# A two-layer decoder step on one core: the turning of queries and keys one unit later, class scores in one round, and near scores of blocks 4 to 7 with 32 stationary columns in four column groups

## The chip, the cores and the metric

The kernel runs on 1 core of one Trainium2 chip. The metric is the time on the device of one execution, in microseconds; lower is better. Engines are named as in the profile: PE is TensorE (PEld its weight loads), DVE is VectorE, ACT is ScalarE, POOL is GpSimd, SP is SyncE, which starts the DMAs.

## The reference

Two layers are applied to a prompt of 1024 tokens and to 8 single tokens of a sample group, with a model width of 1024, 8 attention heads and 8 mLSTM heads of 64 each. Per layer:

```
h = rmsnorm(x); z = h @ w_in            # q, k, v of 8 attention heads, q, k, v, gate of 8 mLSTM heads
for (window, dilation) in ((128, 1), (512, 4), (2048, 16)):
    s = q @ k.T * HEAD_DIM ** -0.5      # keys at distance 0 .. window, in steps of dilation
    m = max(s); e = exp(s - m); l = sum(e); o = e @ v / l
o_a = the three o, merged by their denominators
h_b = chunkwise mLSTM with matrix memory
x += concat(rmsnorm(o_a), sigmoid(o_gate) * rmsnorm(h_b)) @ w_out
x += ConvGLU(rmsnorm(x)); x += sigmoid(rmsnorm(x) @ w_ple_gate) * (p @ w_ple_proj)
```

The change touches `s = q @ k.T` of the prompt and the steps that bring q and k into the layout which it needs.

## The kernel before

Everything stays in one program; each engine has its own list of instructions, written out by hand in Python, and they meet through counting semaphores. There is no scheduler: the order on an engine is the order in which its function issues.

**Products.** The combined projection `h @ w_in` is made for one pair of heads at a time. For pair p there are nine tiles of tokens (eight of 128 prompt tokens, and one with the 8 sample tokens) and eight k-steps each, so 72 k-steps. A k-step is three matmuls over split operands (L1001, L1002, L1003: low times high, high times low, high times high); for the ninth tile of most pairs it is two small ones (L1010, L1012). ScalarE copies a finished tile out of PSUM into `zt` (`z_evac`), which raises `z_done`.

**Attention.** Pairs 0 to 3 hold attention heads. The loop `for p in range(PAIRS): for u in range(NU)` runs over 16 units per pair. Unit u stands for query block u // 2 (128 tokens) and head u % 2 of the pair, so even units have e = 0 and odd ones e = 1. While the units of pair p run, the 72 k-steps of pair p + 1 are dealt out over them (`FILL`: 8, 8, 8, then 4 each, 2 in the last two units), in two halves around the attention steps. In an odd unit PE first issues `scores` of the next query block, for both heads. Then come products, `turn_back` (L1191) and, at the end, `turn_p` (L1160); in an even unit products, `turn_p` and `values` (L1179, L1184) of the block before.

**Scores.** Query blocks 0 to 3 are scored against all keys up to their own block (L1150). Blocks 4 to 7 are scored against two near blocks of 128 keys (L1150, 256 columns) and against class keys: every fourth key, queries and keys sorted into four residue classes. Each class is a matmul with 32 stationary columns (queries) that writes 32 partitions (L1145); four classes and two heads make a round of eight. `class_keys` is 128 for blocks 4 and 5, 224 for block 6 and 256 for block 7, and a round takes at most 128 of them. `q3` is stored with the 128 queries of a block sorted by class, so a slice of 32 is one class; `k3` is stored in order and read with `r:P:4`. The operands are fp32, and each matmul leaves two records in the trace.

**From scores to values.** VectorE adds the mask and takes the maximum (`masked`, L2172, L2174), ScalarE makes the exponentials (`probabilities`, L1690), PE turns them (`turn_p`), VectorE copies them back (`near`, L2182), PE multiplies by the values. `scores` waits for `s_masked`, `turn_p` for `p_done` and for `pt0` of the unit before.

**Norm and turn.** Before `scores` of pair p, its q and k are normed, rotated and turned by PE (`turn_third`, L1106), a third of the eight tiles at a time: thirds 0 and 1 (three tiles each) during the units of the pair before, third 2 (two tiles) during its own. `norm_part` gives VectorE's three steps of the norm (`norm_squares`, `norm_scale`, `norm_rope`, the last instruction of which is L2095) to units 4 to 6 for third 0 and 9 to 11 for third 1. `turn_part` gives the turn of q (j = 0) and that of k (j = 1) to a unit each; in an even unit the turn stands between the two halves of the products, in an odd one at the unit's end. Both use PSUM bank 3. The q turn waits for `qk_norm` and until the bank is emptied of the k turn before (`k_evac`, VectorE's copy L2103); the k turn waits until ScalarE's copy of q (L1679, `q_evac`) is done.

Of the kernel before, what the change touches and what calls it, by code (L numbers as in the profile page):

```python
# [16 lines left out]
P = 128  # L17
# [9 lines left out]
HD = 64  # L27
# [28 lines left out]
def tok(t):  # L56
    return slice(t * P, t * P + rows(t))
# [7 lines left out]
def col(c):  # L65
    return slice(c * CH, (c + 1) * CH)
# [75 lines left out]
def class_keys(qb):  # L142

    return 0 if qb < NDENSE else P if qb < 6 else 32 * (qb + 1)


def near_keys(qb):

    return range(qb + 1) if qb < NDENSE else range(qb - 1, qb + 1)
# [13 lines left out]
def score_bank(g):  # L163

    return g % 3
# [31 lines left out]
def turn_part(p, u):  # L197

    if p == 0 and u in (2, 3):
        return 0, 1, u - 2  # L200
    if u in (6, 7):
        return p, 2, u - 6
    if p + 1 < PAIRS:
        for x, a in enumerate((8, 12)):
            if u in (a, a + 1):
                return p + 1, x, u - a
    return None
# [7 lines left out]
def turned_value(p, half):  # L215

    return 3 * p + half + 1 if p < PAIRS else 3 * PAIRS + 2 * (p - PAIRS) + half + 1
# [61 lines left out]
def tiles(first, last):  # L279
# [9 lines left out]
    s_ready=32, s_masked=64, p_done=64, t0_ready=64, pt0=64, o_ready=32, oc_done=32, ob_ready=32, o_read=32,  # L289
# [45 lines left out]
def build(nc, A, O):  # L335
    with ExitStack() as ctx:
# [3 lines left out]
        def sem(name):  # L340
            return ctx.enter_context(nc.semaphore(name))
# [88 lines left out]
        ps = ctx.enter_context(nc.psum_tensor("ps", [P, 8, 512], F32))  # L430
# [24 lines left out]
        def score_mask(qb):  # L455
# [24 lines left out]
        s_ready, s_masked, p_done, t0_ready, pt0, o_ready, oc_done, ob_ready, o_read = [sem(n) for n in (  # L480
            "s_ready", "s_masked", "p_done", "t0_ready", "pt0", "o_ready", "oc_done", "ob_ready", "o_read")]
# [126 lines left out]
        def one_hot(h, n, g=0):  # L608

            return ident[32 * g:32 * g + NH, 32 * g + h:32 * g + h + 1].to_broadcast([NH, n])  # L610

        def row_part(g, j):

            return rowr[32 * g:32 * g + NH, j * 512:(j + 1) * 512]
# [384 lines left out]
        def _(pe):  # L999
            def three(out, a_hi, a_lo, b_hi, b_lo, first, last):  # L1000
                nc.tensor.matmul(out, a_lo, b_hi, start=first, stop=False)  # L1001
                nc.tensor.matmul(out, a_hi, b_lo, start=False, stop=False)  # L1002
                return nc.tensor.matmul(out, a_hi, b_hi, start=False, stop=last)  # L1003
# [47 lines left out]
            for t in range(5):  # L1051
                turn_x(t)
                if t == 1:
                    n = DEPTH * 3 * KT
# [5 lines left out]
            for l in range(DEPTH):  # L1060
# [69 lines left out]
                def scores(p, qb):  # L1130

                    if qb % 3 == 0:
                        pe.wait_ge(*at(q_evac, turned_value(p, qb // 3)))
                        pe.wait_ge(*at(k_evac, turned_value(p, qb // 3)))
                    g = NU * p + 2 * qb
                    if g >= 2:
                        pe.wait_ge(*at(s_masked, g - 1))
                    q3, k3 = qkA[p % 2]
                    n = class_keys(qb)
                    for a in range(0, n, P):  # L1140
                        b = min(n, a + P)
                        for r in range(4):
                            for e in range(2):
                                h = slice(HD * e, HD * e + HD)
                                mm = nc.tensor.matmul(ps[32 * r:32 * r + 32, score_bank(g + e), a:b].rearrange("p (t i) -> p t i", i=32),  # L1145
                                                      q3[h, qb, 32 * r:32 * r + 32], k3[h, a // 32:b // 32, r:P:4], start=True, stop=True)
                    own = near_keys(qb)
                    for e in range(2):
                        h = slice(HD * e, HD * e + HD)
                        mm = nc.tensor.matmul(ps[:, score_bank(g + e), n:n + len(own) * P].rearrange("p (t n) -> p t n", n=P), q3[h, qb, :],  # L1150
                                              k3[h, own.start:own.stop, :], start=True, stop=True)
                    mm.then_inc(s_ready, 1)
# [59 lines left out]
                products(0, KT * NT + 4, NPROD)  # L1212
                pe.wait_ge(*at(z_done, NT))
                scores(0, 0)
                pe.wait_ge(*at(k_evac, 1))
                for p in range(PAIRS):
                    for u in range(NU):
                        e, qb = UNITS[u]
                        if e and qb + 1 < NT:
                            scores(p, qb + 1)  # L1220
                        elif e and p + 1 < PAIRS:
                            scores(p + 1, 0)
                        part = turn_part(p, u)
                        before = (p, qb - 1) if qb else (p - 1, NT - 1)
                        half = (ahead(u) + ahead(u + 1)) // 2
                        products(p + 1, ahead(u), half)
                        if e == 0:
                            if part:
                                turn_third(*part)
                            products(p + 1, half, ahead(u + 1))  # L1230
                            turn_p(p, u)
                            if before[0] >= 0:
                                values(*before)
                        else:
                            if half == ahead(u + 1):
                                turn_p(p, u)
                            if before[0] >= 0:
                                turn_back(*before)
                            if half < ahead(u + 1):
                                products(p + 1, half, ahead(u + 1))  # L1240
                                turn_p(p, u)
                            if part:
                                turn_third(*part)
# [48 lines left out]
                for q in range(PAIRS):  # L1292
                    p = PAIRS + q
# [39 lines left out]
                    for e in range(2):  # L1333
                        for j in range(2):
                            mm = nc.tensor.matmul(ps[HD * e:HD * e + HD, 3 + j, :], one_hot(2 * q + e, HD, j), row_part(j, j),
                                                  start=True, stop=True)
# [5 lines left out]
                    for j in range(2):  # L1342
                        for e in range(2):
                            mm = nc.tensor.matmul(ps[:, ((0, 1), (2, 5))[e][j], :], one_hot(2 * q + e, P, 2 * e + j),
                                                  row_part(2 * e + j, j), start=True, stop=True)
# [7 lines left out]
                    for c in range(NT):  # L1353
                        g = NT * q + c
                        next_products(ahead_b(q, c), ahead_b(q, c + 1))
                        pe.wait_ge(*at(ws_done, g + 1))
                        if c >= 2:
                            pe.wait_ge(*at(c_upd, 9 * q + c))
                        mm = nc.tensor.matmul(ps[:, (2, 5)[c % 2], 0:2 * (HD + 1)],
                                              att[:, 3 * SEQ + 512 + (c % 2) * P:3 * SEQ + 512 + (c % 2 + 1) * P],  # L1360
                                              zt[:, p % 2, c, VO:OG], start=True, stop=True)
# [4 lines left out]
                        if q + 2 == PAIRS and c == 0:  # L1366
                            pe.wait_ge(*at(kq_used, 3 * NB))
                            for r in range(3):
                                mm = nc.tensor.transpose(ps[0:HD, 0, (r + 1) * P:(r + 2) * P], sall[:, r, :, :].rearrange("p b h -> p (b h)"), ident[:, :])
# [5 lines left out]
                        for e in range(2):  # L1375
                            zc = VO + e * (HD + 1)
                            a = 3 * SEQ + (c % 2) * 256 + e * P
                            nc.tensor.matmul(ps[:, 3 + c % 2, e * (HD + 1):(e + 1) * (HD + 1)], att[:, a:a + P],  # L1378
                                             zt[:, p % 2, c, zc:zc + HD + 1], start=(e == 0), stop=False)
                        if q + 1 == PAIRS and c + 1 == NT:  # L1380
# [3 lines left out]
                                         Cst, start=False, stop=True).then_inc(n_ready, 1)  # L1384
# [31 lines left out]
                for c in range(3):  # L1416
# [3 lines left out]
                    for o in range(KT):  # L1420
# [7 lines left out]
                        for k in range(KT):  # L1428
                            w_h, w_l = weights(B + B_OUT + o // 2, k, 256, (o % 2) * P, P)
                            mm = three(ps[:, 4 + j % 3, 0:CH], w_h, w_l, hi[:, k, col(c)], lo[:, k, col(c)], k == 0, k == KT - 1)  # L1430
# [80 lines left out]
                for j in range(24):  # L1511
                    b, c, o = j // 6, (j % 6) // 2, j % 2
# [8 lines left out]
                    for k in range(KT):  # L1521
                        w_h, w_l = weights(B + B_PLE + 2 * b, k, 256, o * P, P)
                        mm = three(ps[:, j % 3, 0:CH], w_h, w_l, hi[:, k, col(c)], lo[:, k, col(c)], k == 0, k == KT - 1)
# [10 lines left out]
                    for k in range(2):  # L1534
                        w_h, w_l = weights(B + B_PLE + 2 * b + 1, k, 256, o * P, P)
                        mm = three(ps[:, 3 + j % 3, 0:CH], w_h, w_l, ph[:, k, col(c)], pl[:, k, col(c)], k == 0, k == 1)
# [5 lines left out]
            for t in range(NT + 1):  # L1542
# [4 lines left out]
                for k in range(KT):  # L1547
                    mm = nc.tensor.transpose(ps[0:m, 2 * (t % 2) + k // 4, (k % 4) * P:(k % 4 + 1) * P], X[:, k, tok(t)], ident[:, :])
# [1206 lines left out]
```

## Time and profile before

| | us |
|---|---|
| median of 3 runs | 3154.49 |
| lowest and highest | 3153.2, 3158.83 |
| the profiled execution, its own time | 3152.16 |
| its span in the trace | 3150.4 |
| TensorE (PE) busy | 3071.9 (98%) |
| VectorE (DVE) busy | 1823.9 (58%) |
| ScalarE (ACT) busy | 982.0 (31%) |
| mean granted TensorE clock, share of full speed | 0.993 |

The durations below come from that one execution. Its own time is 2.3 us under the median of the runs, its span another 1.8 us less, since the span goes from the first instruction to the last one alone. The attention part of the first layer lies at about 70 to 345 us of the span, that of the second at 1622 to 1900 us.

### The profile page before, as it was taken

What the parts mean: (1) busy time and instruction counts of PE and PEld (TensorE: products, weight loads), DVE (VectorE), ACT (ScalarE), POOL (GpSimd) and SP (SyncE); (2) the same over time, 40 slices, a digit from 0 to 9 for tenths busy, and PEclk for the clock granted to TensorE, in tenths of its full rate; (3) what the DMA queues carried; (4) which work ended last, traced back from release to release, by engine and by line L of the source; (5) the groups of instructions that cost most, each with busy time, mean ns of one, the idle gap of its engine ahead of it and who ended that gap; (6) DMA issues with size and microseconds to landing.
All of it is one profiled execution on the core that took longest, in us unless ns stands there. A gap on an engine that the chain in (4) does not pass through costs nothing.

```text
span 3150.4 us, 52020 instructions
## 1 busy us (share of the span) xinstructions
PE 3071.9 (98%) x20099; PEld 2809.9 (89%) x20099; DVE 1823.9 (58%) x4369; ACT 982.0 (31%) x2053; POOL 899.0 (29%) x2061
## 2 busy tenths in 40 slices
PE   7999999899999999999999999998999999999998
PEld 7877677599999999999997777767999999999998
DVE  5675465755555555557577745646555555555663
ACT  4333244533111111115333333454321111111251
POOL 3112023414223233223422211323223243223231
PEclk8999999999999999999999999999999999999999
DMA  6222133611111111110231222336111111111111
GB/s 186 71 62 55 46 101 112 198 44 63 43 41 41 55 53 41 54 41 24 94 88 49 58 55 59 115 103 191 54 41 41 66 43 46 49 41 41 41 38 72
DMA packets 242335, 213.95 MB, mean 68 GB/s; under 512 B 41988, under 2 KB 221124, under 8 KB 240496
## 3 DMA queue, kind: packets, MB, share of 16 engines
q1 hardware_dynamic: 242088, 210.62, 22.0%
q8 instruction: 159, 2.61, 0.3%
q14 instruction: 88, 0.72, 0.1%
HBM read 178.95 MB, written 31.61 MB: 67 GB/s over the span
## 4 chain that ended last, share of the span: by engine, by line
PE 85%; DVE 9%; ACT 2%; issue 1%; DMA 1%; SPq 1%; POOL 0%; DVEq 0%; ACTq 0%
PE ps L1001 25%; PE ps L1003 25%; PE ps L1002 25%; PE ps L1184 1%; PE ps L1160 1%; DVE att L2182 1%; PE ps L1150 1%; PE ps L1145 1%; PE ps L1179 1%; PE ps L1281 1%; PE ps L1305 1%; DVE lo L2017 1%; DVE att L2172 1%; PE ps L1378 1%; DVE zt L2088 1%
## 5 line engine op out<-in xcount | busy, mean ns | idle before, releaser
L946 POOL TENSOR_TENSOR wlo<-raw,whi 128x128 fp32r<-128x128 f32 (+3 forms) x1952 | 855.4, 484 | 1780.5 <-ACT whi L1570 1382.2
L1001 PE MATMUL ps<-hi,wlo 128*128 128x344 f32 x2880 | 924.3, 321 | 1.9 <-DVE X L2522 1.3
L1003 PE MATMUL ps<-hi,whi 128*128 128x344 f32 x2880 | 919.5, 319 | 0.0
L1002 PE MATMUL ps<-lo,whi 128*128 128x344 f32 x2880 | 918.6, 319 | 0.0
L1001 PEld LDWEIGHTS ps<-hi,wlo 128*128 128x128 f32 x2880 | 541.6, 188 | 5.0 <-issue 2.2
L1003 PEld LDWEIGHTS ps<-hi,whi 128*128 128x128 f32 x2880 | 541.1, 188 | 0.0
L1002 PEld LDWEIGHTS ps<-lo,whi 128*128 128x128 f32 x2880 | 540.2, 188 | 0.6
L1001 PE MATMUL ps<-whi,lo 128*128 128x512 f32 (+3 forms) x1056 | 413.7, 392 | 6.5 <-ACT zt L1645 4.5
L1003 PE MATMUL ps<-whi,hi 128*128 128x512 f32 (+3 forms) x1056 | 390.4, 370 | 0.0
L1002 PE MATMUL ps<-wlo,hi 128*128 128x512 f32 (+3 forms) x1056 | 389.0, 368 | 0.0
L2601 DVE TENSOR_TENSOR X<-X,ps 128x344 f32<-128x344 f32 x528 | 268.3, 512 | 184.5 <-PE ps L1003 182.6
L1912 ACT ACTIVATE wb<-wb 128x344 f32<-128x344 f32 x132 | 64.9, 492 | 967.3 <-DVE wb L2588 967.3
L1001 PE MATMUL ps<-yhi,wlo 128*128 128x344 f32 x1056 | 339.9, 322 | 0.7 <-DVE X L2601 0.7
L1003 PE MATMUL ps<-yhi,whi 128*128 128x344 f32 x1056 | 338.3, 320 | 0.0
L1002 PE MATMUL ps<-ylo,whi 128*128 128x344 f32 x1056 | 337.4, 319 | 0.0
L1001 PEld LDWEIGHTS ps<-whi,lo 128*128 128x128 f32 (+1 forms) x1056 | 197.1, 187 | 68.5 <-issue 26.2
L1003 PEld LDWEIGHTS ps<-whi,hi 128*128 128x128 f32 (+1 forms) x1056 | 196.8, 186 | 26.6
L2580 DVE TENSOR_TENSOR wa<-ps,rstd 128x344 f32<-128x344 f32 x132 | 68.2, 517 | 258.1 <-PE ps L1003 257.7
L1002 PEld LDWEIGHTS ps<-wlo,hi 128*128 128x128 f32 (+1 forms) x1056 | 197.8, 187 | 20.2
L1570 ACT ACTIVATE whi<-raw 128x2048 fp32r<-128x2048 f32 (+3 forms) x106 | 188.1, 1782 | 43.1 <-DMA raw<-in_w_down 33.3
L1001 PEld LDWEIGHTS ps<-yhi,wlo 128*128 128x128 f32 x1056 | 198.7, 188 | 1.5 <-DVE X L2601 1.3
L1002 PEld LDWEIGHTS ps<-ylo,whi 128*128 128x128 f32 x1056 | 198.3, 188 | 0.2
(331 smaller groups left out, 3746.7 us busy)
## 6 DMA issues: line engine op xcount, KB each, us to landing
raw<-in_w_up SPq DMA_DIRECT2D x44, 1024.0 KB, 5.0
raw<-in_w_in SPq DMA_DIRECT2D x112, 256.0 KB, 4.3
raw<-in_w_down SPq DMA_DIRECT2D x22, 1024.0 KB, 4.8
kvb<-in_cache_win_k SPq DMA_DIRECT2D x48, 256.0 KB, 3.0
cache<-in_cache_win_v SPq DMA_DIRECT2D x42, 256.0 KB, 4.0
X<-x_scratch SPq DMA_DIRECT2D x4, 2064.0 KB, 11.5
raw<-in_w_out SPq DMA_DIRECT2D x8, 1024.0 KB, 8.9
raw<-in_w_ple_gate SPq DMA_DIRECT2D x8, 1024.0 KB, 4.9
```

What stands on the lines that cost most here:

```text
L946: pool.tensor_tensor(out=wlo[:, s, r], in0=raw[:, s, r], in1=whi[:, s, r].bitcast(F32), op=ALU.subtract).then_inc(w_split, 1)
L1001: nc.tensor.matmul(out, a_lo, b_hi, start=first, stop=False)
L1002: nc.tensor.matmul(out, a_hi, b_lo, start=False, stop=False)
L1003: return nc.tensor.matmul(out, a_hi, b_hi, start=False, stop=last)
L1145: mm = nc.tensor.matmul(ps[32 * r:32 * r + 32, score_bank(g + e), a:b].rearrange("p (t i) -> p t i", i=32), q3[h, qb, 32 * r:32 * r + 32], ...
L1150: mm = nc.tensor.matmul(ps[:, score_bank(g + e), n:n + len(own) * P].rearrange("p (t n) -> p t n", n=P), q3[h, qb, :], k3[h, own.start:own ...
L1160: mm = nc.tensor.transpose(ps[0:n, 4, j * P:(j + 1) * P], score_place(g)[:, a:a + n], ident[:, :])
L1179: nc.tensor.matmul(ps[HD * e:HD * e + HD, 6, 32 * r:32 * r + 32], class_values(c, r)[0:n, e * HD:(e + 1) * HD], turned_place(g + e)[0:n, a ...
L1570: do(nc.scalar.activation(whi[:, s, 0:used], raw[:, s, 0:used], ACT.Copy), w_hi, wait=False)
L1912: do(nc.scalar.activation(w, w, ACT.Gelu_apprx_tanh), gelu_done, wait=False)
L2580: do(v.tensor_tensor(out=w[:, 2:CH + 2], in0=ps[:, s % 3, 0:CH], in1=rstd[:, col(c)], op=ALU.mult), gate_read)
L2601: do(v.tensor_tensor(out=x, in0=x, in1=ps[:, 5 + (24 * i + j) % 3, 0:CH], op=ALU.add), dn_read, wait=False)
```

## The change

Three edits. The turns of thirds 0 and 1 of the next pair's q and k go from units 8 and 9, 12 and 13 to units 9 and 10, 13 and 14. In `scores`, the class keys of a query block go through in one round of up to 256 columns, where there was one round for each 128. And for query blocks 4 to 7 the near scores are made by eight matmuls, each with the 32 queries of a class as stationary columns, where there were two with all 128; the moving columns, the 256 near keys, stay the same for all of them, and so does what is written where.

```diff
--- before.py
+++ after.py
@@ -201,7 +201,7 @@
     if u in (6, 7):
         return p, 2, u - 6
     if p + 1 < PAIRS:
-        for x, a in enumerate((8, 12)):
+        for x, a in enumerate((9, 13)):
             if u in (a, a + 1):
                 return p + 1, x, u - a
     return None
@@ -1137,14 +1137,21 @@
                         pe.wait_ge(*at(s_masked, g - 1))
                     q3, k3 = qkA[p % 2]
                     n = class_keys(qb)
-                    for a in range(0, n, P):
-                        b = min(n, a + P)
+                    if n:
                         for r in range(4):
                             for e in range(2):
                                 h = slice(HD * e, HD * e + HD)
-                                mm = nc.tensor.matmul(ps[32 * r:32 * r + 32, score_bank(g + e), a:b].rearrange("p (t i) -> p t i", i=32),
-                                                      q3[h, qb, 32 * r:32 * r + 32], k3[h, a // 32:b // 32, r:P:4], start=True, stop=True)
+                                nc.tensor.matmul(ps[32 * r:32 * r + 32, score_bank(g + e), 0:n].rearrange("p (t i) -> p t i", i=32),
+                                                 q3[h, qb, 32 * r:32 * r + 32], k3[h, 0:n // 32, r:P:4], start=True, stop=True)
                     own = near_keys(qb)
+                    if n:
+                        for r in range(4):
+                            for e in range(2):
+                                h = slice(HD * e, HD * e + HD)
+                                mm = nc.tensor.matmul(ps[32 * r:32 * r + 32, score_bank(g + e), n:n + len(own) * P].rearrange("p (t n) -> p t n", n=P),
+                                                      q3[h, qb, 32 * r:32 * r + 32], k3[h, own.start:own.stop, :], start=True, stop=True)
+                        mm.then_inc(s_ready, 1)
+                        return
                     for e in range(2):
                         h = slice(HD * e, HD * e + HD)
                         mm = nc.tensor.matmul(ps[:, score_bank(g + e), n:n + len(own) * P].rearrange("p (t n) -> p t n", n=P), q3[h, qb, :],
```

On PE's queue, at the end of unit 13 and in unit 14 of pair 0, this stood before (L1160 is `turn_p`, L1010 and L1012 the ninth tile's products, L1106 the turn, here that of k):

```order
L1012 MATMUL ps<-wlo,hi 8x384
L1160 MATMUL ps<-ident,att 128x128
L1160 MATMUL ps<-ident,att 96x128
L1160 MATMUL ps<-ident,att 128x128 x2
L1106 MATMUL ps<-ident,zt 128x128 x3
L1010 MATMUL ps<-whi,thin 40x384
L1012 MATMUL ps<-wlo,hi 8x384
L1010 MATMUL ps<-whi,thin 40x384
L1012 MATMUL ps<-wlo,hi 8x384
```

The same place now (the later lines of the file are 7 further down, so `turn_p` is L1167):

```order
L1012 MATMUL ps<-wlo,hi 8x384
L1167 MATMUL ps<-ident,att 128x128
L1167 MATMUL ps<-ident,att 96x128
L1167 MATMUL ps<-ident,att 128x128 x2
L1106 MATMUL ps<-ident,zt 128x128 x3
L1010 MATMUL ps<-whi,thin 40x384
L1012 MATMUL ps<-wlo,hi 8x384
L1106 MATMUL ps<-ident,zt 128x128 x3
L1010 MATMUL ps<-whi,thin 40x384
L1012 MATMUL ps<-wlo,hi 8x384
```

The first L1106 is now the turn of q, which stood in the middle of unit 12 before, and the second, one k-step behind it, is the turn of k.

The scores of query block 7 of pair 0 on PE, with the last values ahead of them (L1184 and L1179 are `values`, L1145 the class scores, L1150 the near scores), before:

```order
L1160 MATMUL ps<-ident,att 128x128 x2
L1184 MATMUL ps<-att,zt 64x128 x2
L1179 MATMUL ps<-att 64x32 x8
L1184 MATMUL ps<-att,zt 64x128 x2
L1145 MATMUL ps<-zt 32x128 x16
L1150 MATMUL ps<-zt 128x256 x2
L1010 MATMUL ps<-whi,thin 40x384
```

And now (L1191 and L1186 are `values`, L1144 the class scores, L1151 the near scores):

```order
L1167 MATMUL ps<-ident,att 128x128 x2
L1191 MATMUL ps<-att,zt 64x128 x2
L1186 MATMUL ps<-att 64x32 x8
L1191 MATMUL ps<-att,zt 64x128 x2
L1144 MATMUL ps<-zt 32x256 x8
L1151 MATMUL ps<-zt 32x256 x8
L1010 MATMUL ps<-whi,thin 40x384
```

Two rounds of class scores with 128 keys became one with 256, and the two near matmuls of 128 stationary columns became eight of 32.

## Rows read from the trace of the kernel before

**Rows 1.** The page: TensorE's busy time, share and instructions.
```profile
PE 3071.9 (98%) x20099; PEld 2809.9 (89%) x20099; DVE 1823.9 (58%) x4369; ACT 982.0 (31%) x2053; POOL 899.0 (29%) x2061
```

**Rows 2.** Busy time by stretch: span, PE, PEld, DVE, ACT, POOL, clock, DMA.
```profile
70.00:345.00 275.00, 264.43 (x2233) 212.09 (x2232) 174.05 (x513) 99.44 (x266) 60.75 (x142) 0.99 0.22 58
```

**Rows 3.** PE's waits: what waited for whom, us in total, times, longest.
```profile
PE ps L1106 <- DVE zt L2095: 10.6, 6, 1.8
...
PE ps L1106 <- DVE zt L2103: 6.6, 4, 2.0
...
PE ps L1106 <- DVE kT L2103: 2.4, 2, 1.2
```

**Rows 4.** Timeline of PE, unit 12 of pair 1: start, duration, instruction.
```profile
194.31 0.33 PE L1003 MATMUL ps<-whi,hi 128*128 128x384 f32 x1
196.41 0.55 PE L1106 MATMUL ps<-ident,zt 128*128 128x128 f32 x3 [1.77 <-DVE zt L2095]
196.72 0.42 PE L1001 MATMUL ps<-whi,lo 128*128 128x384 f32 x1
```

**Rows 5.** Timeline of PE, unit 8 of pair 0.
```profile
110.80 0.34 PE L1003 MATMUL ps<-whi,hi 128*128 128x384 f32 x1
...
112.72 0.42 PE L1001 MATMUL ps<-whi,lo 128*128 128x384 f32 x1
```

**Rows 6.** Timeline of PE, around a q turn that waits for nobody.
```profile
88.27 0.34 PE L1003 MATMUL ps<-whi,hi 128*128 128x384 f32 x1
...
88.69 0.42 PE L1001 MATMUL ps<-whi,lo 128*128 128x384 f32 x1
```

**Rows 7.** Timeline of PE, unit 8 of pair 2.
```profile
243.24 0.34 PE L1003 MATMUL ps<-whi,hi 128*128 128x384 f32 x1
...
245.85 0.42 PE L1001 MATMUL ps<-whi,lo 128*128 128x384 f32 x1
```

**Rows 8.** Timeline of PE, end of unit 13 and unit 14 of pair 1.
```profile
203.09 0.49 PE L1106 MATMUL ps<-ident,zt 128*128 128x128 f32 x3
203.33 0.42 PE L1010 MATMUL ps<-whi,thin 128*40 128x384 f32 x1
...
203.77 0.33 PE L1010 MATMUL ps<-whi,thin 128*40 128x384 f32 x1
```

**Rows 9.** Timeline of ACT: its copy of the q turn of rows 4.
```profile
197.00 0.49 ACT L1679 ACTIVATE zt<-ps 128x384 f32<-128x384 f32 x1 [3.42 <-PE ps L1106]
```

**Rows 10.** Timeline of DVE: near(7) of pairs 0 and 2, near(12) of pair 2.
```profile
111.28 0.69 DVE L2182 COPY att<-ps 128x512 f32<-128x512 f32 x1
...
244.41 0.69 DVE L2182 COPY att<-ps 128x512 f32<-128x512 f32 x1
...
268.17 0.69 DVE L2182 COPY att<-ps 128x512 f32<-128x512 f32 x1 [2.37 <-PE ps L1184]
```

**Rows 11.** Busy time by stretch, behind the stall of pair 2 (columns as rows 2).
```profile
246.00:250.00 4.00, 4.00 (x26) 3.39 (x25) 1.86 (x6) 1.94 (x5) 4.00 (x10) 0.57 0.02 4
```

**Rows 12.** Timeline of PE, scores of blocks 5 and 7 of pair 1.
```profile
180.45 1.09 PE L1184 MATMUL ps<-att,zt 128*64 128x128 f32 x16
181.48 0.66 PE L1145 MATMUL ps<-kT,rstd 64*32 64x128 f32 x16
182.07 0.70 PE L1150 MATMUL ps<-kT,rstd 64*128 64x256 f32 x4
182.70 0.44 PE L1001 MATMUL ps<-whi,lo 128*128 128x384 f32 x1
...
199.43 1.12 PE L1145 MATMUL ps<-kT,rstd 64*32 64x128 f32 x32
200.48 0.70 PE L1150 MATMUL ps<-kT,rstd 64*128 64x256 f32 x4
```

**Rows 13.** Timeline of PE, scores of block 3 of pair 0 (512 columns).
```profile
98.34 1.13 PE L1150 MATMUL ps<-zt 64*128 64x512 f32 x4
99.40 0.44 PE L1001 MATMUL ps<-whi,lo 128*128 128x384 f32 x1
```

## Prediction

> **What bounds the kernel now.** I read the page first: TensorE is busy for 98% of the span [rows 1], so a change counts where it takes work or idle time off TensorE. The changed lines run in the attention part of each of the two layers alone; in the first that is 70 to 345 us, where PE is busy 264.43 of 275 us, so 10.6 us idle [rows 2]. The table of waits says before what it idles: L1106, the turning of a third of q or k, waited 10.6 + 6.6 + 2.4 = 19.6 us in 12 waits, each time for VectorE [rows 3]. That is nearly all of PE's idle time in both attention parts. The timeline shows where. In unit 12 of pair 1 (the q turn of third 1) PE issues its last product at 194.31, L1106 starts at 196.41, released by the rope step L2095, and the next product at 196.72 [rows 4]. In unit 8 of pair 0 (third 0) it is 110.80 to 112.72 [rows 5]; there the wait is for the copy L2103 that empties bank 3.
>
> **The change, part by part. (a) Later turns.** A q turn that waits for nobody takes, from the last product before it to the first behind it, 88.69 - 88.27 = 0.42 us [rows 6]. The stalled ones take 196.72 - 194.31 = 2.41 and 112.72 - 110.80 = 1.92 us, and the one in unit 8 of pair 2 takes 245.85 - 243.24 = 2.61 us [rows 7]: 1.99, 1.50 and 2.19 us too much. A layer has three of the first kind, two like the second, one like the third: 3 x 1.99 + 2 x 1.50 + 2.19 = 11.2, and two layers 22.3 us. (It is more than 19.6 because a restart costs 0.2 us beyond the idle time that the table counts.) Are the operands there later? The rope step was done 2.1 us after PE had got to unit 12; the new place, the end of unit 13, where the k turn stands now, lies at 203.09, 6.7 us behind the old one [rows 4, 8]. Third 0 moves as far, and was 1.5 to 2.2 us short. Yes, with much to spare.
>
> What is late next? First, the k turn. It needs bank 3 emptied by ScalarE, and it now stands in the middle of unit 10 or 14, close behind its q turn. ScalarE's copy starts 0.04 us after the turn ends (196.41 + 0.55, then 197.00) and takes 0.49 [rows 4, 9]; with 0.04 for the hand-over back, the bank is free 0.57 us after a turn's end. In unit 10 two k-steps stand in between, six products of 384 columns, at 2.4 GHz at least 0.96 us: no wait. In unit 14 it is one k-step of the ninth tile, two matmuls from 203.33 to 203.77, beside a turn whose modelled end is 203.09 + 0.49 = 203.58 [rows 8]. So the k turn is up at 203.77 and may start at 203.58 + 0.57 = 204.15. That is 0.38 us of wait; 0.11 of it would have gone into its own fill (0.42 us unstalled against 196.72 - 196.41 = 0.31), so 0.27 is lost, in 3 pairs of 2 layers 1.6 us (bounds 0, if the copy hides, and 3.2, at twice that). Behind it in PE's queue wait turn_p(14) and the values of block 6, and near(14) on VectorE waits for turn_p. VectorE's copy of k moves ahead of near(14), whose input comes later anyway.
>
> Second, VectorE. In pair 2 PE would reach turn_p(8), which needs near(7), seven products behind 243.24, at 244.36; near(7) ends at 244.41 + 0.69 = 245.10 [rows 7, 10]: 0.7 us of stall remain, 1.4 in two layers (bounds 0 and 2.8). In pair 0 PE would be there at 110.80 + 1.12 = 111.92, and near(7) ends at 111.28 + 0.69 = 111.97: nothing to speak of. Behind the stall of unit 12 VectorE waits 2.37 us for PE (268.17) [rows 10], so PE may come 2 us earlier there, and the k copy that moves down by a unit (about 0.5 us) fits as well.
>
> Third, the clock. Behind the stall of pair 2 the granted clock is 0.57 over 246 to 250 us [rows 11], a stretch at 1.2 instead of 2.4 GHz; (1 - 0.57) x 4 = 1.7 us of full-speed work went there. Without the idle time ahead of it I count that as gained (bounds 0 and 1.7).
>
> (a) sums to -22.3 + 1.6 + 1.4 - 1.7 = -21.0 us.
>
> **(b) Class scores in one round.** Block 7 has 256 class keys, two rounds now, block 6 has 224. A block with one round of 128 takes 182.07 - 181.48 = 0.59 us, the two rounds of block 7 take 200.48 - 199.43 = 1.05 [rows 12]: 0.46 for 128 columns more, 3.6 ns each, and 0.59 - 0.46 = 0.13 us constant. So the second round costs about what its columns cost, if the streaming bounds it. One round of 256 has the same columns: 0 us, though 128 fewer matmuls are issued. Bounds: 0, and a whole constant saved in each of 16 merged blocks, -2.1.
>
> **(c) Near scores with 32 stationary columns.** Now two matmuls of 256 columns take 182.70 - 182.07 = 0.63 us [rows 12], of 512 columns 99.40 - 98.34 = 1.06 [rows 13]. So 256 columns are 0.43 us (four passes at 2.4 GHz with both heads side by side) and 0.20 is a constant, the change of form and the first load of 128 columns. Afterwards eight matmuls stream the 256 columns in eight tiles, right behind class rounds of the same form, whose constant is paid already. The two ends: if all eight tiles stream side by side at full rate, near costs 0.43, that is 0.20 less; if they run at the class rounds' rate, 256 x 3.6 ns = 0.92, 0.29 more. The trace has no near score of this form. The class rounds take 3.6 ns a column where full rate would be 1.67, and differ from L1150 in two ways: eight tiles instead of two, and keys read at every fourth element instead of in a row. That the reading is at fault is suggested by L1184, which splits the array into two column groups and reads unbroken rows: its 16 records, eight matmuls of four passes of 128 columns, take 181.48 - 180.45 = 1.03 us [rows 12], and two full-rate streams would need 0.85. I take -0.20 in 4 blocks x 4 pairs x 2 layers = 32 blocks: -6.4 us; the other end is +9.3.
>
> The Trainium skill, "SBUF — State Buffer", Specifications (TRN2), says that a 16-byte line must be hit at least twice for full bandwidth; every fourth fp32 element hits each line once. By that rule the class rounds are slow through their stride and the near rounds would not be: the sum would be the one I take. By the class row alone it would be 15.7 us longer.
>
> Sum: -21.0 + 0 - 6.4 = -27.4 us on the profiled execution's 3152.16, so 3124.8. The median shown, 3154.49, is 2.3 higher: 3127.
>
> **Rivals.** R1: eight tiles don't keep full rate, (c) is +9.3, and the time 3154.5 - 21.0 + 9.3 = 3143. For it: the only rounds of this form in the trace run at that rate. Against it: the stride.
> R2: the stall moves. Units 8 and 12 are freed, but turn_p, turn_back or the k turns wait for VectorE or ScalarE in its place, and half of (a) comes back, 10 us: 3137. For it: the 0.7 us of pair 2. Against it: VectorE's idle 2.37 us behind the old stall.
> R3, slower: the four column groups of the near scores, which all read the same key columns, stream one after the other. Then near costs 4 x 0.43 + 0.1 = 1.8 us instead of 0.63, 32 x 1.18 = +38 us: 3154.5 - 21.0 + 38 = 3171. It decides once near takes over 0.63 + 21.0/32 = 1.29 us. Against it: eight class matmuls of four passes of 128 columns would need 0.85 us in that way, and take 0.46 beside their constant.
>
> **How the numbers follow.** Forecast 60% (its own range 3121 to 3134), R1 23%, R2 12%, R3 3%, others 2%. The range for 8 in 10 has to reach R1: 3119 to 3145. Two tenths of a per cent, what a measurement here can tell from no change, are 6.3 us, so faster means below 3148, which holds for the forecast, R2 and most of R1: 0.92; same 0.05 (R1 together with R2); slower 0.03.
>
> **What would show it.** L1106's waits fall from 19.6 us to under 4, all in unit 14 and ended by ScalarE. From the first class record to the first product behind the near scores it is 0.59 + 0.63 = 1.22 us for a block with 128 class keys: 1.02 by the forecast, 1.5 by R1, 2.4 by R3; for block 7, 1.68: 1.5, 2.0, 2.9. The drop of the clock at 246 us is gone. I am wrong in (a) if L1160 or L1191 wait more than 3 us more, in (c) if the scores take longer than now.

## The result, and the profile after

The changed kernel takes 3132.88 us (median of 4 runs, 3131.01 to 3135.49), the one before in the same comparison 3155.98 (median of 4, 3153.2 to 3158.83). The ratio is 0.993, its 95% interval 0.9917 to 0.9942: 22 us faster by the ratio, 23.1 by the medians. The forecast was 3127, with 3119 to 3145 as the range.

The page of the profiled execution: span, then busy time, then the chain that ended last by engine.

```profile
span 3133.7 us, 52276 instructions
...
PE 3068.3 (98%) x20227; PEld 2808.6 (90%) x20227; DVE 1824.9 (58%) x4369; ACT 980.6 (31%) x2053; POOL 900.0 (29%) x2061
...
PE 88%; DVE 6%; ACT 2%; DMA 2%; issue 1%; SPq 1%; POOL 0%; DVEq 0%; ACTq 0%
```

PE's busy time fell by only 3.6 us against [rows 1], the span by 16.7; most of what went was idle time. The two attention parts, busy time by stretch (columns as in [rows 2]):

```profile
70.00:335.00 265.00, 262.58 (x2315) 212.14 (x2315) 175.94 (x516) 99.23 (x267) 61.76 (x140) 1.00 0.23 60
1617.00:1883.00 266.00, 263.51 (x2352) 211.95 (x2351) 174.98 (x515) 99.82 (x268) 56.17 (x128) 1.00 0.23 60
```

PE is idle 2.4 us of 265, where it was 10.6 of 275 [rows 2]. Measured from the first turn of a layer (L1106) to the first instruction behind its attention part, the part takes 276.7 us instead of 290.0 in the first layer and 276.8 instead of 288.6 in the second, 25.0 us less in all. That is more than the 16.7 us by which the profiled spans differ. Some 8 us of this one execution went elsewhere. The first turn started 2.5 us later. From the end of the first attention part to the first turn of the second layer 5.5 us more passed; in that stretch PE waited 4.9 us at once for L2404, which stood behind a load of in_state_C (2.1 us before, and at most 2.4 to 4.0 us in other kernels here that don't change that code). The other 2.7 us of the stretch are not traced to a cause. The medians, 23.1 us apart, don't show that loss.

PE's waits, whole run (who waited for whom, us in total, times, longest):

```profile
PE ps L1366 <- DVE att L2404: 9.2, 4, 4.9
...
PE ps L1167 <- DVE att L2189: 1.7, 2, 0.8
...
PE ps L1106 <- ACT rstd L1686: 0.9, 4, 0.2
...
PE ps L1106 <- ACT zt L1686: 0.5, 2, 0.2
```

The 19.6 us of L1106 [rows 3] are 1.4, in six waits, and who ends them is no longer VectorE's norm but ScalarE's copy of q. Beside it stands a new wait: L1167 (`turn_p`) for L2189 (VectorE's `near`), 0.8 us in each layer.

The timeline of PE at the end of unit 13 and in unit 14 of pair 0 (start, duration, instruction), to be laid beside [rows 8]:

```profile
135.16 0.49 PE L1106 MATMUL ps<-ident,zt 128*128 128x128 f32 x3
135.40 0.41 PE L1010 MATMUL ps<-whi,thin 128*40 128x384 f32 x1
135.66 0.34 PE L1012 MATMUL ps<-wlo,hi 128*8 128x384 f32 x1
136.23 0.55 PE L1106 MATMUL ps<-ident,zt 128*128 128x128 f32 x3 [0.23 <-ACT rstd L1686]
136.54 0.42 PE L1010 MATMUL ps<-whi,thin 128*40 128x384 f32 x1
```

The q turn ends at 135.65 and the k turn starts at 136.23, 0.58 us later. From the last product before the k turn to the first behind it, it is 136.54 - 135.66 = 0.88 us, against 0.42 for an unhindered turn [rows 6]: 0.46 us lost, though the table counts 0.23 of it as idle.

The scores of block 5 and of block 7 of pair 0, the new form of [rows 12] (L1144 class, L1151 near):

```profile
116.10 0.67 PE L1144 MATMUL ps<-zt 64*32 64x128 f32 x16
116.54 0.66 PE L1151 MATMUL ps<-zt 64*32 64x256 f32 x16
117.13 0.45 PE L1001 MATMUL ps<-whi,lo 128*128 128x384 f32 x1
...
131.69 1.12 PE L1144 MATMUL ps<-zt 64*32 64x256 f32 x16
132.59 0.66 PE L1151 MATMUL ps<-zt 64*32 64x256 f32 x16
133.18 0.37 PE L1010 MATMUL ps<-whi,thin 128*40 128x384 f32 x1
```

117.13 - 116.10 = 1.03 us for block 5, 1.22 before; 1.49 for block 7, 1.68 before. The near matmuls, 256 columns, take 0.59 us including the way back to the products' form (the form is the tile of rows x stationary columns that a matmul uses), while the class round of the same 256 columns takes 0.90.

### The profile page after: what moved, and what is told of

It reads as the page before. It is cut to its first block, busy times and chain, and to the rows that moved or that the text cites. A ratio compares the mean times of both kernels' runs of the same rounds, so it can differ in the third digit from the quotient of the medians.

```text
span 3133.7 us, 52276 instructions
## 1 busy us (share of the span) xinstructions
PE 3068.3 (98%) x20227; PEld 2808.6 (90%) x20227; DVE 1824.9 (58%) x4369; ACT 980.6 (31%) x2053; POOL 900.0 (29%) x2061
## 4 chain that ended last, share of the span: by engine, by line
PE 88%; DVE 6%; ACT 2%; DMA 2%; issue 1%; SPq 1%; POOL 0%; DVEq 0%; ACTq 0%
PE ps L1001 26%; PE ps L1003 25%; PE ps L1002 25%; PE ps L1191 1%; PE ps L1167 1%; PE ps L1144 1%; PE ps L1113 1%; PE ps L1186 1%; PE ps L1312 1%; DVE lo L2024 1%; PE ps L1288 1%; PE ps L1385 1%; PE ps L1157 1%; DMA kvb<-in_cache_win_k 1%; PE ps L1010 0%
```

## The experiments

Times are medians, each with the median of the kernel before in its own comparison. "Score blocks" are the mean times of blocks 4, 5, 6 and 7, from the first record of the scores to the first behind them, as in [rows 12]; the kernel before has 1.23, 1.23, 1.58 and 1.69 us, the changed one 1.04, 1.03, 1.37 and 1.48.

**The later turns alone.**

```diff
-        for x, a in enumerate((8, 12)):
+        for x, a in enumerate((9, 13)):
```

> The later turns alone, scores as before. Theory (the terms add up: the two traces give 24.9 us for both attention parts, of which 6.4 us are the score blocks and 1.7 us the clock): 16.8 to 18.5 us under the kernel before, near 3138; PE's waits at L1106 1.4 us in 6 waits, all in unit 14, and a wait of about 1.7 us of L1160 for VectorE in unit 8 of pair 2. Rival A (the score change made most of the room for the turns): less than 12 us. Rival B (the score change costs time elsewhere and the turns gave all): 23 us or more.

3136.73 against 3156.15 us, ratio 0.994 (0.9928 to 0.9953). L1106 waits 1.4 us in 6 waits for ScalarE, L1160 1.2 us for VectorE. The interval allows a gain of 14.8 to 22.7 us. Rival A (less than 12) is out, and rival B (23 or more) lies just outside. The time lies 1 us beyond the theory's best, well inside what the interval leaves open.

**The new scores alone**, turns as before (the change's diff without its first hunk).

> The new scores alone, turns in units 8, 9, 12 and 13 as before. The score blocks themselves take 1.04, 1.03, 1.37 and 1.48 us as in the changed kernel, 6.4 us less in all. Theory (the stalls of units 8 and 12 end when VectorE is done, whatever PE saved ahead of them, so blocks 4 and 6, which stand right ahead of them, give nothing in pairs 0 to 2): the gain is 6.4 less up to 12 x 0.2 = 2.4 us, so 4.0 us, and L1106's waits rise from 19.6 towards 22 us. Rival (VectorE's steps hang on the scores and move with them): the whole 6.4 us, L1106's waits at 19.6.

3151.68 against 3156.15 us, ratio 0.9987 (0.9978 to 0.9996). The waits of PE at the turns (who waited for whom, us in total, times, longest):

```profile
PE ps L1106 <- DVE zt L2102: 11.4, 7, 1.8
...
PE ps L1106 <- DVE zt L2110: 7.4, 4, 2.2
...
PE ps L1106 <- DVE kT L2110: 2.8, 2, 1.4
```

They are 21.6 us instead of 19.6. Of the 2.0 us more, 0.85 are a wait of the first turn of the second layer, in a place that none of the edits touches. The other 1.2 us are what PE saved ahead of a stall and waited away in it. I compared the starts of `turn_p` in all 128 units with those of the kernel before. In units 8, whose stall waits for a copy at the end of VectorE's own chain, the 0.2 us saved in unit 7 came back as 0.2 us of stall, in six units. In units 12 they did not: the stall there ended earlier with PE, so VectorE's rope step moved up too. So the truth lies between the two: 5.3 us instead of 6.4 or 4.0. (These 5.3 are twice the gain of the second layer, which ran at full clock in both traces. The median and its interval, 1.3 to 6.9 us of gain, can't tell the two apart.)

The execution also bears on the clock. Busy time by stretch around the stall of pair 2 in the first layer, which is 2.21 us long here:

```profile
242.00:246.80 4.80, 2.63 (x18) 2.27 (x16) 4.56 (x13) 1.53 (x3) 3.18 (x6) 1.00 0.00 0
246.80:250.80 4.00, 3.96 (x61) 3.10 (x61) 3.08 (x8) 2.06 (x6) 3.79 (x9) 1.00 0.00 0
```

The granted clock stayed at 1.00, where [rows 11] had 0.57 behind the same stall. The next two kernels, which keep that stall too, show no drop there either. Nor does the second layer of the kernel before, with the same stall of 1.98 us (L1106 at 1797.68) in the very execution that the prediction was made from:

```profile
1795.00:1798.00 3.00, 1.02 (x8) 0.73 (x7) 2.86 (x9) 1.65 (x3) 1.18 (x4) 1.00 0.00 0
1798.00:1802.00 4.00, 4.00 (x48) 2.88 (x47) 2.83 (x9) 1.94 (x5) 4.00 (x10) 1.00 0.02 6
```

**Only the near scores in the new form**, class scores in rounds of 128, turns as before.

```diff
-                    if n:
+                    for a in range(0, n, P):
+                        b = min(n, a + P)
                         for r in range(4):
                             for e in range(2):
...
-                                                 q3[h, qb, 32 * r:32 * r + 32], k3[h, 0:n // 32, r:P:4], start=True, stop=True)
+                                                 q3[h, qb, 32 * r:32 * r + 32], k3[h, a // 32:b // 32, r:P:4], start=True, stop=True)
```

(against the new scores alone)

> Only the near scores with 32 stationary columns; class scores in rounds of 128, turns as before. Theory (the gain of the score blocks is the constant of the near matmuls alone, a merged round saves nothing): score blocks 1.04, 1.03, 1.38 and 1.49 us, within 0.02 us of those with merged rounds, and the time equal to that of the new scores alone within 1 us. Rival (the merged round saves its own constant of 0.13 us): blocks 6 and 7 are 0.13 us longer than in the changed kernel, 2 us in all.

3153.59 against 3156.15 us, ratio 0.9988 (0.9979 to 0.9997). Score blocks 1.04, 1.04, 1.38 and 1.49 us: with merged rounds blocks 6 and 7 are 0.01 us shorter, not 0.13. The medians of this kernel and of the one with all new scores are 1.9 us apart, their ratios 0.0001; to tell 1 us, as the theory has it, the intervals are too wide, so it is the score blocks that decide.

**Only the class scores in one round**, near scores and turns as before: the first part of the hunk in `scores`.

> Only the class scores in one round; near scores with 128 stationary columns, turns as before. Theory: 0 us, score blocks of 1.23, 1.23, 1.58 and 1.68 us as in the kernel before (within 0.03). Rival (a merged round saves 0.13 us): 1.45 and 1.55 us for blocks 6 and 7, 2 us under the kernel before.

3156.45 against 3156.15 us, ratio 0.9997 (0.9988 to 1.0006). Score blocks 1.23, 1.23, 1.57 and 1.68 us. The merged round is worth 0.2 us in 32 blocks; it changes nothing that can be measured.

**Class keys read in a row.** On the changed kernel:

```diff
-                                                 q3[h, qb, 32 * r:32 * r + 32], k3[h, 0:n // 32, r:P:4], start=True, stop=True)
+                                                 q3[h, qb, 32 * r:32 * r + 32], k3[h, 0:n // 32, 0:32], start=True, stop=True)
```

> The changed kernel, but the class scores read the first 32 keys of each block in a row, not every fourth one. This changes the computation (wrong keys, the same number of columns and of matmuls). Theory (the stride halves the rate, 3.6 against 1.67 ns a column): 736 class columns a pair at 1.93 ns less each, score blocks 0.79, 0.79, 0.94 and 0.99 us instead of 1.04, 1.03, 1.37 and 1.48, so 11.4 us less on PE and a time of about 3122 to 3124. Rival (the rate is that of eight small tiles with keys of their own each, stride or not): score blocks and time as in the changed kernel.

3124.76 against 3154.83 us, ratio 0.9903 (0.989 to 0.9917). Score blocks 0.81, 0.81, 0.97 and 1.02 us. Block 7 of pair 0:

```profile
130.81 0.66 PE L1144 MATMUL ps<-zt 64*32 64x256 f32 x16
131.27 0.64 PE L1151 MATMUL ps<-zt 64*32 64x256 f32 x16
131.84 0.37 PE L1010 MATMUL ps<-whi,thin 128*40 128x384 f32 x1
```

The same 16 records of 256 columns take 0.46 us instead of 0.90. Besides the step between the elements one thing differs: the four classes now read the same keys, where each had its own. The last kernel below tells the two apart.

**Near keys read at every fourth element**, on the changed kernel; the counterpart.

```diff
-                                mm = nc.tensor.matmul(ps[32 * r:32 * r + 32, score_bank(g + e), n:n + len(own) * P].rearrange("p (t n) -> p t n", n=P),
-                                                      q3[h, qb, 32 * r:32 * r + 32], k3[h, own.start:own.stop, :], start=True, stop=True)
+                                mm = nc.tensor.matmul(ps[32 * r:32 * r + 32, score_bank(g + e), n:n + len(own) * P].rearrange("p (z t i) -> p z t i", z=2, i=32),
+                                                      q3[h, qb, 32 * r:32 * r + 32], k3[h, 0:4, r:P:4].unsqueeze(1).to_broadcast([HD, 2, 4, 32]), start=True, stop=True)
```

> The changed kernel, but its near scores stream 256 columns read at every fourth element (128 keys of blocks 0 to 3, twice over). This changes the computation, with the same number of columns and matmuls. Theory (stride): near costs 256 x 3.6 = 0.92 us instead of 0.43, score blocks 1.53, 1.52, 1.86 and 1.97 us, 32 x 0.49 = 15.7 us more, a time of about 3148. Rival (it is not the stride): as the changed kernel.

3146.64 against 3154.83 us, ratio 0.9972 (0.9962 to 0.9981); score blocks 1.51, 1.51, 1.86 and 1.96 us. Block 5 of pair 0:

```profile
115.45 0.67 PE L1144 MATMUL ps<-zt 64*32 64x128 f32 x16
115.89 1.12 PE L1151 MATMUL ps<-zt 64*32 64x256 f32 x16
116.95 0.44 PE L1001 MATMUL ps<-whi,lo 128*128 128x384 f32 x1
```

Near takes 1.06 us instead of 0.59. Here too each class now reads keys of its own, where all four read the same.

**Near keys read at every second element**, likewise.

```diff
-                                mm = nc.tensor.matmul(ps[32 * r:32 * r + 32, score_bank(g + e), n:n + len(own) * P].rearrange("p (t n) -> p t n", n=P),
-                                                      q3[h, qb, 32 * r:32 * r + 32], k3[h, own.start:own.stop, :], start=True, stop=True)
+                                mm = nc.tensor.matmul(ps[32 * r:32 * r + 32, score_bank(g + e), n:n + len(own) * P].rearrange("p (t i) -> p t i", i=64),
+                                                      q3[h, qb, 32 * r:32 * r + 32], k3[h, qb - 3:qb + 1, 0:P:2], start=True, stop=True)
```

> The changed kernel, but its near scores read every second element of four key blocks, 256 columns as before. This changes the computation. Theory (a 16-byte line hit twice keeps full rate): score blocks as in the changed kernel, 1.04, 1.03, 1.37, 1.48 us, and the same time. Rival (every stride costs, in proportion to the lines touched): near at 1.5 times, 0.64 us, 0.21 more a block, 6.7 us in all.

3135.17 against 3154.83 us, ratio 0.9935 (0.992 to 0.995); score blocks 1.06, 1.06, 1.40 and 1.51 us, 0.02 to 0.03 more than in the changed kernel. A step of two is nearly free, a step of four is not. All four classes read the same keys in this kernel; a step of two with keys of their own was not run.

**The k turn of third 1 in unit 15**, on the changed kernel.

```diff
-            if u in (a, a + 1):
-                return p + 1, x, u - a
+            if u in (a, a + 1 + x):
+                return p + 1, x, int(u > a)
```

> The changed kernel with the k turn of third 1 at the end of unit 15 instead of in the middle of unit 14. Theory (there the bank is long empty): the interval from turn_p(13) to turn_p(14), 0.57 us longer in the changed kernel than before, loses that wait; L1106 waits for nobody, and 6 x 0.46 = 2.8 us are gained. Rival (the copy of k on VectorE comes too late for the next pair, whose third 2 needs the bank, or delays the first masks of that pair): new waits of PE in units 0 to 3, no gain or a loss.

3131.91 against 3154.83 us, ratio 0.9922 (0.991 to 0.9935). L1106 waits for nobody any more. By the starts of `turn_p`'s weight loads, the interval from unit 13 to 14 is 0.57 us shorter, from 14 to 15 0.12 shorter, and from 15 to the next pair's unit 0, where the turn now stands, 0.33 longer: 0.35 us in each of 6 pairs, 2.1 us. The theory holds at three quarters of its size; a difference of 2 us from the changed kernel is below what the intervals resolve.

**VectorE's norm of third 0 in units 5 to 7**, on top of it.

```diff
-        for x, a in enumerate((4, 9)):
+        for x, a in enumerate((5, 9)):
```

> As the kernel with the k turn in unit 15, and VectorE's three norm steps of third 0 go from units 4 to 6 to units 5 to 7. Theory (what is left of the stall of unit 8 in pair 2, 0.8 us of L1167 for VectorE's copy near(7) in each layer, comes from the rope step that stands ahead of that copy): the wait is gone, 2 x 0.85 us and the restart are gained, about 2 us, near 3130. Rival (the rope step then delays VectorE's work of unit 8, the mask and copies that PE needs next): the wait goes to unit 8 or 9 and the time stays or grows.

3135.49 against 3157.33 us, ratio 0.9934 (0.992 to 0.9947). The wait of L1167 for VectorE is gone, and another has come (these lines had 1.5 us in 8 waits before this edit):

```profile
PE ps L1198 <- DVE oa L2193: 7.4, 12, 2.2
```

The timeline of VectorE in units 7 and 8 of pair 2 (start, duration, instruction):

```profile
236.61 0.69 DVE L2189 COPY att<-ps 128x512 f32<-128x512 f32 x1
...
237.55 0.95 DVE L2095 TENSOR_TENSOR zt<-zt,qkg 128x768 f32<-128x768 f32 x1
...
243.65 0.28 DVE L2193 COPY oa<-ps 128x128 f32<-128x128 f32 x1
```

`near(7)` (L2189) is on time, but the rope step and the squares now lie between it and the copies of unit 8, and in unit 9 `turn_back` waits 2.2 us for L2193; in pair 1 it waits 0.7 us. The rival was right. Against the kernel without this edit the medians of the two comparisons are 3.6 us worse; the intervals alone would not settle that, the new waits do.

This execution also has the drop of the clock again, behind the new stall of pair 2 in the first layer (PE stands still up to 243.98), and not behind the equal one of the second layer:

```profile
244.00:248.00 4.00, 4.00 (x17) 3.90 (x18) 1.81 (x7) 1.16 (x4) 1.75 (x5) 0.58 0.22 54
```

**Keys stored by class**, on top of the kernel with the k turn in unit 15. It leaves nothing out.

```diff
-                                                 q3[h, qb, 32 * r:32 * r + 32], k3[h, 0:n // 32, r:P:4], start=True, stop=True)
+                                                 q3[h, qb, 32 * r:32 * r + 32], k3[h, 0:n // 32, 32 * r:32 * r + 32], start=True, stop=True)
...
-                                mm = nc.tensor.matmul(ps[32 * r:32 * r + 32, score_bank(g + e), n:n + len(own) * P].rearrange("p (t n) -> p t n", n=P),
-                                                      q3[h, qb, 32 * r:32 * r + 32], k3[h, own.start:own.stop, :], start=True, stop=True)
+                                mm = nc.tensor.matmul(ps[32 * r:32 * r + 32, score_bank(g + e), n:n + len(own) * P].rearrange("p (t i r) -> p t r i", i=32, r=4),
+                                                      q3[h, qb, 32 * r:32 * r + 32], k3[h, own.start:own.stop, :].rearrange("p t (r i) -> p t r i", r=4), start=True, stop=True)
...
-                    do(v.tensor_copy(k3, src), k_evac, wait=False)
+                    do(v.tensor_copy(k3.rearrange("p t (r i) -> p t r i", r=4), permuted(src)), k_evac, wait=False)
```

(and the near scores of blocks 0 to 3 in the same way)

> As the kernel with the k turn in unit 15, but VectorE stores k sorted by class, as q is, so that the class scores read their keys in a row. The near scores (and those of blocks 0 to 3) read in a row too and write their columns to PSUM at every fourth element, back in the order of the keys. Nothing is left out. If strided writes cost nothing: class scores at 1.67 ns a column, score blocks 0.81, 0.81, 0.97 and 1.02 us, 10 us less, near 3122. If a strided write halves the rate like a strided read: blocks 4 to 7 at 1.3, 1.3, 1.46 and 1.5 us and blocks 0 to 3 up from 0.42, 0.63, 0.85, 1.06 by 0.21, 0.43, 0.64 and 0.85, some 17 us for these and 2 to 5 us for the others more, near 3150.

3122.56 against 3157.33 us, ratio 0.9892 (0.9878 to 0.9905). Block 3 and block 7 of pair 0:

```profile
100.61 1.13 PE L1157 MATMUL ps<-zt 64*128 64x512 f32 x4
101.67 0.44 PE L1001 MATMUL ps<-whi,lo 128*128 128x384 f32 x1
...
130.85 0.66 PE L1144 MATMUL ps<-zt 64*32 64x256 f32 x16
131.31 0.64 PE L1151 MATMUL ps<-zt 64*32 64x256 f32 x16
131.87 0.37 PE L1010 MATMUL ps<-whi,thin 128*40 128x384 f32 x1
```

Block 3 takes 1.06 us, as with unbroken writes [rows 13], the class round of block 7 0.46 and its near scores 0.56. Score blocks 0.81, 0.81, 0.97 and 1.02 us. The class round reads keys of its own for each class, as in the changed kernel, and is as fast as with shared ones: it is the step that costs. The kernel beats the changed one and the one with the k turn in unit 15, the latter by 9 us by the medians; the score blocks are 10.4 us shorter, and L1167's waits for VectorE grow from 1.6 to 2.9 us.

## Why the prediction was right, and where its terms were off

The mechanism held, and the time lies inside the forecast's own range of 3121 to 3134, near its slow end. Four terms were too favourable and none clearly the other way, so the forecast does not rest on errors that cancel.

**The bound.** That PE's time counts, and that its idle time in attention stands ahead of L1106, held: with the turns moved, 8 us of idle time left the first attention part.

**(a) Later turns, forecast -21.0 us; alone they measured -19.4 us (3136.73 - 3156.15).** The mechanism is right, and the size nearly. Three of its terms were off.
- The k turn in unit 14: the place and the releaser are as forecast, and 0.58 us from the end of the q turn to the k turn against my 0.57. The loss is 0.46 us, not 0.27: I subtracted the fill of the turn as if the wait hid it, but a stalled turn takes 0.31 us for itself, an unhindered one 0.42 - 0.17 = 0.25 (0.17 is the last product's own share). So 0.38 of wait would have been 0.44 lost. It makes 2.8 us in six turns instead of 1.6. The kernel with the k turn in unit 15 agrees: its two intervals around unit 14 lose 0.57 + 0.12 = 0.69 us, which are the turn itself, 0.25, and 0.44.
- What is left in unit 8 of pair 2: 0.8 us a layer against 0.7.
- The clock: the 1.7 us were counted as the price of the stall. The traces of five kernels have ten stalls of 2.0 to 2.2 us in their attention parts, and the granted clock falls behind two of them (the kernel before and the one with the norm in units 5 to 7, both in the first layer); the attention parts of the seven kernels without such a stall are at 1.00 throughout. So in these attention parts the drop came only behind such a stall, and seldom. The term should have been a fraction of 1.7 us, with 1.7 as its bound, and the second layer of the same trace, which had the stall and no drop, could have told so. Why it falls behind some and not behind others no run shows.

By the starts of `turn_p`, and without the clock (twice the gain of the second layer, at full clock in both traces), the turns alone gained 18.0 us; my terms without the clock make 19.3, and with the k turn at 2.8 and unit 8 at 1.6 they make 17.9.

**(b) One round, forecast 0.** 0.2 us by the score blocks, nothing by the times. A round's cost is its columns.

**(c) Near scores, forecast -6.4 us.** The score blocks of the changed kernel are 6.4 us shorter, 45.8 against 39.3 for all 32. The choice between the two ends was open in the trace, and the reading of the keys settles it: class columns at 3.6 ns fall to 1.8 once their elements lie in a row (0.46 us for 256), near columns rise by 0.47 us a block once they are read at every fourth element. Eight tiles side by side are no limit. What the 0.20 us consist of, the change of form or the first load of 128 columns, no run tells apart. What the forecast missed is where the gain is paid out: alone it is 5.3 us, since the 0.2 us of block 4 are waited away in unit 8. With the turns moved it is hardly more, 5.5 us (the changed kernel against the turns alone, by the starts of `turn_p`). The stall is gone, but unit 8 still takes back 0.2 us in pairs 0 to 2: in pair 2 in L1167's wait, 0.8 us instead of 0.6, in pairs 0 and 1 in a later start of L1167 (in pair 0 it stands 0.45 us behind the last product instead of 0.27) that the table of waits does not count. The parts add up: 18.0 + 5.3 = 23.3 us, and both together gained 23.5 without the clock.

**Rivals.** R1 and R3 are out by the score blocks. R2 is out in size: new waits of PE at L1167 and L1106 are 3.1 us, not 10. Its mechanism is real, though: with VectorE's norm of third 0 one unit later the stall came back at `turn_back`.

**The sum.** The forecast median was 3127, the measured one 3132.88, 5.9 us more. The kernel before has 3155.98 in this comparison instead of the 3154.49 that the forecast started from, 1.5 us of the 5.9. The terms account for 4.0: the clock 1.7, the k turn 1.2, block 4 in unit 8 0.9, unit 8 of pair 2 0.2.

## What to carry to other kernels

A stall that ends on another engine's chain can be won back if the waiting step moves to where its operand has long been ready, less what is waited for next (18.0 of 22.3 us here); so look at the pair of steps that share a buffer, since they now stand close together. Pack small matmuls into column groups only with a moving operand that is read in a row or at every second fp32 element (the latter shown for column groups that share their keys); put the permutation into the copy that makes the operand or into the PSUM side of the matmul, where it cost nothing here. A drop of the granted clock at one place of one trace is no full term of a sum: look first whether the other stalls of that length, in the same trace, have it too.

## What the runs showed of the hardware

Eight fp32 matmuls of 64 rows and 32 stationary columns run side by side at full rate: 256 columns take 0.46 us with moving elements in a row, where [rows 12, 13] have 0.43 for 256 columns more in two tiles of 128 stationary columns. With a step of four elements the same takes 0.90 us, with a step of two 0.02 to 0.03 us a block more than in a row. That agrees with the Trainium skill, "SBUF — State Buffer", Specifications (TRN2), where a 16-byte line must be hit twice.

What I had not expected: a matmul that writes its fp32 columns to PSUM at every fourth element is as fast as one that writes them in a row, 1.059 us for a block of 512 columns either way, and the near scores in eight tiles take 0.56 us where unbroken writes take 0.57 (131.84 - 131.27). The Trainium skill, "SBUF — State Buffer", section "Door 1: The DMA port swizzle (why `[64,N]` ≈ `[32,N]`)", says that any non-contiguous PSUM access slows matmuls down significantly; for these writes the measurement says otherwise. VectorE's copy of k with the same permutation, read from PSUM, kept its 0.55 us too.

In the attention parts, stalls of TensorE of 2.0 to 2.2 us were followed by a stretch at a granted clock of 0.57 or 0.58 twice in ten times; the first layer lost 1.5 us by it in the trace of the kernel before (the gain of the changed kernel there is 13.2 us by the starts of `turn_p`, 11.8 in the second layer).
